# Opening loads on two queues with TensorE at work on zeros, and router logits with the router columns held

## The reference, cut to what matters

```
h = rmsnorm(x, norm1_g)                  # 512 x 1024
proj = h @ w_in                          # 1024 x 3584; f, q, v, g of HGRN2, q, k, v of attention
... HGRN2 recurrence, dilated attention, head norms
x = x + concat([o_a, o_b]) @ w_out
h2 = rmsnorm(x, norm2_g)
logits = h2 @ router_w + router_b        # 512 x 32 experts
top 4 of 32, softmax of their logits as gates
x = x + sum over the 4 experts of gate * (clamped_swiglu(h2 @ w_up[e] + b_up[e]) @ w_down[e] + b_down[e])
return rmsnorm(x, final_norm_g)
```

## Time and profile before

| | us |
|---|---|
| median of 3 runs | 1284.49 (1283.56 to 1284.55) |
| the profiled execution, its own time | 1284.0 |
| its span, first to last instruction | 1282.2 |
| TensorE busy | 1245.9 (97%) |
| VectorE busy | 554.7 (43%) |
| ScalarE busy | 238.6 (19%) |
| L1769 (transposes of the opening), 32 records | 7.3 |
| L1967 (logits), 64 records | 7.7 |

### The profile page before, as it was taken

How to read it: one execution, slowest core, us unless ns; L and a number is a source line. 1 busy time by engine, 2 the same in 40 slices (tenths; PEclk the granted TensorE clock), 3 DMA queues, 4 the chain that set the end, 5 groups by cost and what they waited for, 6 DMA issues and landing times.

```text
span 1282.2 us, 33934 instructions
## 1 busy us (share of the span) xinstructions
PE 1245.9 (97%) x15007; PEld 680.1 (53%) x15008; DVE 554.7 (43%) x1066; ACT 238.6 (19%) x463; POOL 122.7 (10%) x127
## 2 busy tenths in 40 slices
PE   6999999999999999999999999999999999999994
PEld 5888887884455544444444444444444454444442
DVE  5657648665544533333333424233323333332423
ACT  6354436421100001000000001000100000000104
POOL 0000005200110110101010101010110101010001
PEclk9999999999999999999999999999999999999998
DMA  8422208069899999999999999999999999999983
GB/s 241 134 66 82 84 1 331 21 264 423 346 412 380 416 426 419 425 424 423 423 423 424 423 425 423 424 422 425 421 423 423 423 424 424 423 423 424 424 353 144
DMA packets 69547, 444.26 MB, mean 346 GB/s; under 512 B 6537, under 2 KB 35821, under 8 KB 44721
## 3 DMA queue, kind: packets, MB, share of 16 engines
q1 hardware_dynamic: 65696, 433.61, 82.6%
q0 software_dynamic: 3696, 8.38, 1.8%
HBM read 439.10 MB, written 4.72 MB: 346 GB/s over the span
## 4 chain that ended last, share of the span: by engine, by line
PE 92%; DMA 4%; DVE 2%; ACT 1%; issue 1%; SPq 0%; DVEq 0%
PE psum L2081 43%; PE psum L2098 20%; PE psum L1807 9%; PE psum L2153 6%; PE psum L1804 3%; DMA w_raw_pair<-w_down 3%; PE psum L2072 2%; PE psum L1892 2%; PE psum L1950 1%; PE psum L1925 1%; PE psum L2129 1%; PE psum L1967 1%; DMA shape_consts<-shape_constants 1%; PE psum L1769 1%; PE psum L1905 1%
## 5 line engine op out<-in xcount | busy, mean ns | idle before, releaser
L2081 PE MATMUL psum<-w_raw_pair,x_slots_turned 128*32 128x512 f32 x4928 | 551.0, 594 | 2.0 <-DVE x_slots_turned L1649 0.7
L2081 PEld LDWEIGHTS psum<-w_raw_pair,x_slots_turned 128*32 128x32 f32 x4928 | 168.5, 110 | 317.7 <-issue 296.9
L1584 DVE TENSOR_TENSOR x_rows<-x_rows,psum 128x1024 f32<-128x1024 f32 x120 | 141.1, 1217 | 330.7 <-PE psum L2153 330.7
L2098 PE MATMUL psum<-w_raw_pair,a_slots 128*32 128x256 f32 x4864 | 272.3, 379 | 1.2 <-DMA w_raw_pair<-w_down 1.1
L2098 PEld LDWEIGHTS psum<-w_raw_pair,a_slots 128*32 128x32 f32 x4864 | 164.9, 110 | 116.0 <-issue 21.8
L889 ACT ACTIVATE lin<-psum 128x768 f32<-128x768 f32 (+1 forms) x32 | 22.5, 704 | 606.3 <-PE psum L2081 606.3
L1553 DVE STREAM_TRANSPOSE a_slots<-glu 128x768 f32<-128x768 f32 (+1 forms) x31 | 26.3, 849 | 183.4 <-PE psum L2098 183.4
L2153 PEld LDWEIGHTS psum<-y_part_group,token_sel 32*128 32x128 f32 x2432 | 76.7, 184 | 48.7 <-issue 48.6
L686 POOL COPY gather_quarters<-row_quarters 128x2 int32 (+1 forms) x30 | 16.5, 550 | 761.1 <-DVE x_slots_turned L1548 704.3
L2153 PE MATMUL psum<-y_part_group,token_sel 32*128 32x256 f32 x2432 | 88.8, 287 | 0.0
L898 ACT ACTIVATE y_part_group<-psum,gate_t 128x256 fp32r<-128x256 f32 x76 | 31.0, 471 | 255.6 <-PE psum L2098 245.0
(11 more groups left out here) (312 smaller groups left out, 990.8 us busy)
## 6 DMA issues: line engine op xcount, KB each, us to landing
w_raw_pair<-w_up SPq DMA_DIRECT2D x128, 2048.0 KB, 26.5
w_raw_pair<-w_down SPq DMA_DIRECT2D x60, 2048.0 KB, 25.5
w_in_raw<-w_in SPq DMA_DIRECT2D x28, 512.0 KB, 3.8
w_raw_pair<-w_down SPq DMA_DIRECT2D x8, 1024.0 KB, 36.6
w_buf<-w_out SPq DMA_DIRECT2D x4, 1024.0 KB, 11.1
x_rows<-x SPq DMA_DIRECT2D x4, 512.0 KB, 5.3
x_rows<-x SPq DMA_DIRECT2D x1, 2048.0 KB, 13.2
normed_rows<-h_rows SPq DMA_DIRECT2D x4, 512.0 KB, 4.5
```

The source lines that it names most:

```text
L1584: dve.tensor_tensor(x_tile, x_tile, PS[:, first_bank:first_bank + 4, half], ALU.add).then_inc(added, 1)
L2081: ins = pe.matmul(U[quarter(j), g, :], slots, up_columns(w, j), start=False, stop=(c == UPC - 1))
L2098: ins = pe.matmul(Yp2[quarter(j), g, :], As[:, g, 2 * c + h, :], raw[q.slot(m)][:, at_w:at_w + 256], start=(c + h == 0 and g % 2 == 0), st ...
```

## The change

**Opening.** Tiles 0 and 2 are loaded from SP's queue, tile 1, the identity and tile 3 from ScalarE's, ahead of its other work. TensorE, once the zeros are in SBUF, makes five f32 products of 128 by 512 zeros into a bank that is written again later; then it transposes the vectors, before the first tile. VectorE copies the vectors behind the scaling of tiles 0 and 1 and ahead of the second pair of scales; before that the copies came behind tile 3.

**Router.** `logit_parts(i)` holds 32 router columns of block k (stationary, 32 columns) and moves the 128 turned rows; block k goes to output quarter k mod 4, so that each quarter has the sum of two blocks, turned (experts by tokens). ScalarE copies the 128x128 to `LG[:, 6, :]`. `logits(i)` is one f32 product of that with a 0/1 matrix of 32 columns, which adds the four quarters and turns the result. For tile i-1 the parts now stand ahead of the last four matmuls of `x2 (i,1)`, and the sum behind them; for the last tile they stand around `first_rows(1)`. ScalarE's copy of half 1 comes ahead of its square of `x2 (i,0)`. The job list gives `lg (2)` a place ahead of `h2T (3,0)`.

```diff
--- before.py
+++ after.py
@@ -58,6 +58,7 @@
 BIAS_ROWS = 3 * NE
 QUARTER = D // 4
 PEELED = 28
+WARM_UP = 5
 AFTER = PEELED
 OVER_PAIR = 3
 FURTHER = -(-(SEQ + STEP) // BLK) - 1
@@ -358,8 +359,8 @@
             before = [("h2T", i - 1, n) for n in range(2) if i]
             places = [("pos",)] if i == TT - 1 else []
             jobs += [("x2", i, 0)] + before + places + [("x2", i, 1)]
-            jobs += [("lg", i - 1)] if 0 < i < TT - 1 else []
-        jobs += [("h2T", TT - 1, 0), ("lg", TT - 2), ("h2T", TT - 1, 1), ("lg", TT - 1)]
+            jobs += [("lg", i - 1)] if i else []
+        jobs += [("h2T", TT - 1, 0), ("h2T", TT - 1, 1), ("lg", TT - 1)]
         number = {name: n for n, name in enumerate(jobs)}
         uses = [len([n for n in range(len(jobs)) if n % 8 == b]) for b in range(8)]
         bank_full = [S(f"bank_full{b}") for b in range(8)]
@@ -511,9 +512,8 @@
         @block.sync
         def _(sp):
             xv = x.rearrange("(t p) d -> p t d", p=P)
-            for i in range(TT):
+            for i in range(0, TT, 2):
                 sp.dma_start(X[:, i, :], xv[:, i, :]).then_inc(S(f"x_in{i}"), 16)
-            sp.dma_start(C[:, 0:2 * P], consts[:, 0:2 * P]).then_inc(S("c_in"), 16)
             sp.dma_start(vec_rows[0:8, :], norm1_g.rearrange("o (k p) -> (o k) p", p=P)).then_inc(S("vec_in"), 16)
             sp.dma_start(vec_rows[8:16, :], lb_logits.rearrange("r (k p) -> (r k) p", p=P)).then_inc(S("vec_in"), 16)
             sp.dma_start(vec_rows[16:20, :], hgrn_g.rearrange("o (k p) -> (o k) p", p=P)).then_inc(S("vec_in"), 16)
@@ -742,6 +742,10 @@
         @block.scalar
         def _(act):
 
+            xv = x.rearrange("(t p) d -> p t d", p=P)
+            act.dma_start(X[:, 1, :], xv[:, 1, :]).then_inc(S("x_in1"), 16)
+            act.dma_start(C[:, 0:2 * P], consts[:, 0:2 * P]).then_inc(S("c_in"), 16)
+            act.dma_start(X[:, 3, :], xv[:, 3, :]).then_inc(S("x_in3"), 16)
             act.wait_ge(S("warm"), 1)
             act.activation(warm[:, 1:2], warm[:, 0:1], ACT.Sqrt).then_inc(S("tables"), 1)
 
@@ -930,19 +934,29 @@
                 act.activation(H2T[:, i % 2, 4 * n:4 * n + 4, :], bank("h2T", i, n).rearrange("p (k m) -> p k m", m=P),
                                ACT.Copy).then_inc(free_sem("h2T", i, n), 1)
 
+            def logit_parts(i):
+
+                act.wait_ge(S("logit_parts"), i + 1)
+                if i:
+                    full(act, "lg", i - 1)
+                act.activation(LG[:, 6, :], bank("lg", i)[:, 0:P], ACT.Copy).then_inc(S("logit_parts_out"), 1)
+
             full(act, "xa", BEHIND_OT)
             act.wait_ge(S("c_rest"), 16)
             bias_row(BSU, of_expert(0), bsu_ready)
             for i in range(TT):
                 for n in range(2):
+                    c = slice(n * 512, (n + 1) * 512)
+                    if i and n == 0:
+                        router_half(i - 1, 1)
                     freed(act, "x2", i, n)
-                    c = slice(n * 512, (n + 1) * 512)
                     act.activation(H2[:, i, c], X[:, i, c], ACT.Square, accum_out=ss2[:, i, n:n + 1]).then_inc(S("ss2"), 1)
                     if i and n == 0:
-                        router_half(i - 1, 1)
+                        logit_parts(i - 1)
                 act.wait_ge(S("mean_eps"), 5 + i)
                 root(act, r2[:, i:i + 1], mean2[:, i:i + 1])
             router_half(TT - 1, 1)
+            logit_parts(TT - 1)
             act.activation(warm[:, 3:4], warm[:, 0:1], ACT.Exp).then_inc(S("tables"), 1)
             act.wait_ge(S("lg_shifted"), 1)
             act.activation(LG[:, 1, :], LG[:, 1, :], ACT.Exp).then_inc(S("lg_exp"), 1)
@@ -1049,13 +1063,14 @@
             dve.wait_ge(S("r1"), 1)
             scaled_rows(0)
             scaled_rows(1)
+            full(dve, "vec")
+            dve.tensor_copy(g2c, bank("vec")[:, 24:32]).then_inc(S("vec_copied"), 1)
+            dve.tensor_copy(vec_T[:, 0:24], bank("vec")[:, 0:24]).then_inc(free_sem("vec"), 1)
             dve.wait_ge(S("ss1"), TT)
             row_scales(slice(2, TT))
             dve.wait_ge(S("r1"), 2)
             scaled_rows(3)
-            full(dve, "vec")
-            link(dve.tensor_copy(g2c, bank("vec")[:, 24:32]))
-            dve.tensor_copy(vec_T, bank("vec")[:, 0:24]).then_inc(free_sem("vec"), 1)
+            dve.wait_ge(S("vec_copied"), 1)
             freed(dve, "vec")
 
             def w_low(c):
@@ -1325,7 +1340,7 @@
                 tile = slice(t * NE, (t + 1) * NE)
                 logit, fourth, allowed, same = LG[:, 0, tile], top8[:, t, TOPK - 1:TOPK], rt[:, 0, t:t + 1], rtmp[:, 8:8 + TOPK]
                 full(dve, "lg", t)
-                dve.scalar_tensor_tensor(logit, bank("lg", t)[:, 0:NE], r2[:, t:t + 1], rb_rows[:, :], ALU.mult, ALU.add
+                dve.scalar_tensor_tensor(logit, bank("lg", t)[:, P:P + NE], r2[:, t:t + 1], rb_rows[:, :], ALU.mult, ALU.add
                                          ).then_inc(free_sem("lg", t), 1)
                 freed(dve, "lg", t)
                 link(dve.max(top8[:, t, :], logit))
@@ -1768,15 +1783,18 @@
             def turned(k, i):
                 return pe.transpose(blocks_of(bank("hT", k))[:, i, :], XN[:, i, k * P:(k + 1) * P], ident)
 
+            pe.wait_ge(S("zero_rows"), 1)
+            for n in range(WARM_UP):
+                pe.matmul(bank("hT", DK - 2), ZR[:, 0:P], ZR[:, 0:SEQ], start=True, stop=True)
             pe.wait_ge(S("c_in"), 16)
+            pe.wait_ge(S("vec_in"), 80)
+            pe.transpose(begin("vec")[:, 0:32], vec_rows[:, :], ident[0:32, 0:32]).then_inc(full_sem("vec"), 1)
             for i in range(2):
                 pe.wait_ge(S("xn"), i + 1)
                 for k in range(DK - 1):
                     if i == 0:
                         begin("hT", k)
                     turned(k, i)
-            pe.wait_ge(S("vec_in"), 80)
-            pe.transpose(begin("vec")[:, 0:32], vec_rows[:, :], ident[0:32, 0:32]).then_inc(full_sem("vec"), 1)
             begin("hT", DK - 1)
             turned(DK - 1, 0)
             turned(DK - 1, 1)
@@ -1938,10 +1956,12 @@
             pe.wait_ge(S("w_out_low"), 4)
             pe.wait_ge(S("router_scaled"), 1)
 
-            def attn_share(i, n):
+            def attn_share(i, n, parts_of=None):
                 o = begin("x2", i, n)
                 s = slice(i * P, (i + 1) * P)
                 for rows, low_w in ((OTH, False), (OTH, True), (OTL, False)):
+                    if rows is OTL and parts_of is not None:
+                        logit_parts(parts_of)
                     if rows is OTL and i + n == 0:
                         for j in range(4):
                             freed(pe, "oT", j)
@@ -1959,13 +1979,20 @@
                     ins = pe.transpose(o[:, k, :], X[:, i, c:c + P], ident)
                 ins.then_inc(full_sem("h2T", i, n), 1)
 
-            def logits(i):
-                o = begin("lg", i)[:, 0:NE]
+            def logit_parts(i):
+
+                o = begin("lg", i)
                 for n in range(2):
                     freed(pe, "h2T", i, n)
                 for k in range(DK):
-                    ins = pe.matmul(o, H2T[:, i % 2, k, :], rw_sb[:, k, :], start=(k == 0), stop=(k == DK - 1))
-                ins.then_inc(full_sem("lg", i), 1)
+                    ins = pe.matmul(o[quarter(k % 4), 0:P], rw_sb[:, k, :], H2T[:, i % 2, k, :], start=(k < 4), stop=(k >= 4))
+                ins.then_inc(S("logit_parts"), 1)
+
+            def logits(i):
+
+                pe.wait_ge(S("logit_parts_out"), i + 1)
+                pe.matmul(bank("lg", i)[:, P:P + NE], LG[:, 6, :], cst("expert_row")[:, 0:NE], start=True, stop=True
+                          ).then_inc(full_sem("lg", i), 1)
 
             def places(t):
 
@@ -1986,11 +2013,11 @@
                 if i == TT - 1:
                     for t in range(TT - 2):
                         places(t)
-                attn_share(i, 1)
+                attn_share(i, 1, i - 1 if i else None)
+                if i:
+                    logits(i - 1)
                 if i == TT - 1:
                     rows_turned(i, 0)
-                if i:
-                    logits(i - 1)
 
             def first_rows(i):
 
@@ -2004,8 +2031,9 @@
 
             rows_turned(TT - 1, 1)
             first_rows(0)
+            logit_parts(TT - 1)
+            first_rows(1)
             logits(TT - 1)
-            first_rows(1)
             places(TT - 2)
             places(TT - 1)
             first_rows(TT - 2)
```

## The result

The change takes 1288.47 us (median of 8 runs, 1287.42 to 1289.4), before 1284.74 (8 runs, 1283.56 to 1285.37): ratio 1.0032, 95% interval 1.0023 to 1.0041 (a ratio here is not the quotient of the two medians, which is 1.0029 for the change). It is 3.7 us slower; the forecast was 1285.0, and the range ended at 1287.6.

A forecast was written before the change was run, and what follows sets the result against it. TensorE, 92% of the chain, was taken to bound the kernel, with VectorE nearly as full in the router stretch. Opening -0.55 plus router +1.1 gave +0.55, so 1285.0 us; range 1282.6 to 1287.6.

The forecast's parts named there:

- both terms: Opening gains 0.55 us (from -1.2 to +0.4); router stretch loses 1.1 us (bounds -4.8 and +3.5).
- rival 2: Opening: clock falls between warm-up and products, first products at half speed, losing 1.9 to 3.8 us: 1287.8; chance 0.14.
- Loads: Opening: second queue changes order, not rate; tile 0 lands at 5.2, third tile scaled at 11.9, nothing gained.
- Warm-up: Opening: five products of zeros raise TensorE's clock at 6.7 and end at 8.9, bounds 6.4 and 11.1.
- First product: Opening: TensorE's first product moves from 17.69 to 17.15, behind h's low part, a gain of 0.5 us.
- Router's order of waits: Router: partial sums wait for VectorE's copy, delaying each second addition; tile 8.38 to 9.19, TensorE idle 2 us, +1.1 in all.
- rival 1: Router: TensorE sets the stretch, so its saving of 4.8 us arrives, with 0.5 from the opening: 1279.2; chance 0.10.

The follow-up runs named there:

- e1_opening: The change's opening alone, with the vectors' transpose and copies moved, on the router of the kernel before: 1284.56 us, ratio 1.0005.
- e6_no_warm_up: The change's opening without its products of zeros, on the router of the kernel before: 1282.97 us, ratio 1.0005.
- e3_opening_fill: The change's opening alone plus a 256-column product of zeros behind each of the first six pairs of last transposes: 1283.47 us, ratio 1.0003.
- e2_router: The change's router part alone, with the opening of the kernel before: 1286.02 us, ratio 1.0022.
- e9_late_no_fill: e5_router_late without its two fill products: 1281.96 us, ratio 0.999 to the kernel before.
- e4_change_fill: The whole change plus six fill products in the opening and two ahead of the last slots: 1285.25 us, ratio 1.0013 to the kernel before.
- e5_router_late: Kernel before with the change's router, partial sums behind the whole addition, sum product and ScalarE's copy moved, two fill products before the last slots: 1281.14 us, ratio 0.9984.
- e7_opening_order: The change's opening with four fill products and the second w_in block's parts behind h's, on the router of the kernel before: 1282.9 us, ratio 1.0002.

## Why the prediction was wrong

It forecast no change, with the signs of both terms argued; the step that failed is rival 2's, which I gave 0.14: "the one fall in the trace came some 4 us behind the last work; the longest gap here is 2.3". A fall at the end of the program, where TensorE had been idle for 4 us, shows that 4 us was enough there, and says nothing of 2.3. In the change and in e1_opening the gap of 2.35 was followed by a fall, and the products were 0.43 apart for over 3 us, the sign that the prediction had named. Rival 2 gave 1287.8. That this is near the 1288.47 measured is in part luck: it had one fall, priced at 1.9 to 3.8, where the profile has two of 1.7, the second in a place that the prediction didn't ask about. The runs put the loss with the router: its part alone is at 1.0022 (1.0013 to 1.0031), some 2.8 us where 1.1 was forecast, while the opening alone can't be told from no change.

- Loads: tile 0 at 5.2, measured 5.86, and 5.7 to 6.1 in six more profiles with this load order; outside my bounds of 4.1 to 5.4. The third tile at 11.9 was 12.24. The Trainium skill (DMA: Bandwidth & Descriptors, "Issuing engines are not separate DMA queues") fits: the four tiles were squared at 5.86, 7.11, 8.60 and 9.83, for 4.10, 5.34, 8.19 and 9.56, so none was squared sooner; only the identity, put ahead, was there before 9.20 for 9.97. A slip of the sum: the 10.5 for tile 3's landing at 330 GB/s leaves out the 0.6 that the 8.6 beside it has, and would be 11.0; the bound it gave wasn't reached.
- Warm-up: end at 8.9, measured 9.27 (in e1_opening the same products took 6.24 us instead of 7.50). It did what it was for, the transposes behind it ran at full speed; e6_no_warm_up shows that nothing was gained by it.
- First product: 17.15, measured 17.64. With the clock kept (e3_opening_fill) the opening is worth -0.10 to the first mark, not -0.55; without, it costs 1.57. The difference, 1.67, is the fall's (priced 1.9 to 3.8), and it rests on the same load order in both. The -0.10 and 1.57 themselves depend on which execution of before they are taken from: with the unchanged opening the first mark was at 255.34 (e2_router), 255.18, 254.15 and 253.79 in four profiles, a spread of 1.55. What the opening is worth apart from the clock is therefore not shown by profiles, and the runs of e3_opening_fill show no change (0.9994 to 1.0012).
- Router's order of waits: right in place and sign. The tile went to 9.32 for the 9.19 said, the choice to +1.40 for +1.1, the idle time to 1.86 for 2. The terms that were small are the partial sums, 0.64 from first start to last end for 0.50, and the four products behind them, 1.20 for 1.07.
- What I left out: my own sum had TensorE idle at the end of the stretch, and I asked about the clock in the opening alone. The gather behind the wait for the last choice lost 1.68 us to it; e9_late_no_fill and e4_change_fill show it from both sides. Of the 4.65 us in the profile the clock took 1.67 + 1.68 = 3.35, the rest of the opening -0.10, and VectorE's order 1.40.
- "TensorE sets the stretch" (rival 1, 1279.2) was wrong for this change, and half right as a possibility: with the sums behind the addition (e5_router_late) 2.0 of its 4.8 us are to be had, until the orders of VectorE and ScalarE set the tile (7.67, in which VectorE waits 0.79 for ScalarE's squares and 0.24 for the sum product).

How often the falls happen can be estimated from the mean granted clock of every run. A fall that costs 1.7 us lowers the mean over 1284 us by 0.0013. The eleven runs of e1_opening have 0.9941 on average and those of e2_router 0.9934, for 0.9947 in the 33 of before beside them: by that estimate a fall in about every second execution, and about one in each. The change's eight have 0.9924 (measured apart from these), near two in each. e3_opening_fill has 0.9948, so its fill leaves nothing to see; e4_change_fill has 0.9939, so some 1.0 of the 1.7 us that its ratio stands for may still be the clock's. Each run's clock is on record to three digits only, so these are rough.

Open: what decides whether a given wait is followed by a fall. It was tile 2 in e2_router, the gather in the change and in e9_late_no_fill. The ratios of the two parts, 1.0005 and 1.0022, sum to less than the change's 1.0032, but well within their intervals.

## What to carry to other kernels

Making an engine faster where another's order sets the pace gives that time back as idleness, and on TensorE idleness can cost twice, by the half clock of what comes next (here 1.67 and 1.68 us behind waits of 2.35 and of 1.92 + 0.64); so for every gap that a change opens, price the work behind it at half speed. Where a cheaper piece needs a new wait, put it behind everything that others wait for: with the partial sums ahead of the last four matmuls of a tile's addition the router part was at 1.0022, with them behind (and the sum and ScalarE's copy moved along) at 0.9990 without fill and 0.9984 with it. Fill products in such a gap, into PSUM that is written again before anyone reads it, kept the clock at 1.00 there in each of the seven profiles that had them; the runs show their worth for both gaps together, 1.0013 for 1.0032.

## What the runs showed of the hardware

- The clock fell to 1.2 GHz behind single waits of 2.35 us (opening of the change) and 1.86 us (e2_router), and behind 1.92 or 1.69 followed by 0.64 us (the gathers of the change and e9_late_no_fill); it stayed at 2.4 GHz behind waits of 1.50 (e5_router_late) and 1.02 (e6_no_warm_up), behind 1.8 (e7_opening_order, ahead of the v block), behind 1.86 in the change's own tile 2, and behind 1.93 followed by 0.64 (e2_router). The length of one wait doesn't decide by itself in these rows. Nor did a fall always come with the first product behind the wait: in e1_opening it came 1.4 us after the products had begun, in e9_late_no_fill 0.8 after the gather had.
- Transposes alone were followed by full speed: in e5_router_late the second 18 transposes took 2.19 us with only transposes before them, where the same code took 4.02 before. The Trainium skill (TensorE: Matmul & The Clock Gate, "Part 4: PE-mode transpose") says that the full clock doesn't engage for transposes; the measurement decides against it here. What is measured is the time of a transpose, 0.12 us for 0.22: the column of the granted clock stands at 1.00 from 8 to 18 us in both profiles, so it shows the later falls and not this slow start.
- The opening of the kernel before varies by itself: the first mark was at 255.18 in its profile, and at 254.15 and 253.79 in e5_router_late and e9_late_no_fill, whose openings are the same code. Most of it is when the loads land: tile 0 was squared at 4.07 to 4.10 in all three, but tile 3 at 9.56, 8.86 and 8.14, and the first product came at 17.69, 16.63 and 16.27. Timeline of e9_late_no_fill, against the earlier trace rows:

```profile
8.14 1.06 ACT L752 ACTIVATE x_sq<-x_rows 128x1024 f32<-128x1024 f32 x1
...
16.27 0.47 PE L1817 MATMUL psum<-h_low,w_in_high 128*128 128x512 f32 x1 [1.50 <-DVE h_low L1087]
```
